# One core of a Trainium2 transformer layer: pooling input moved into the preparation's gap, box sums into the read-out, both directions' low-rank products together

## The chip, the cores and the metric

The kernel runs on one core of a Trainium2 chip. The metric is the device time of one execution in microseconds (us); before the change three executions took 1624.69, 1631.42 and 1635.77 us, median 1631.42.

## What is computed

One layer of a backbone over 512 latent tokens (a grid of 8 rows of 64) with 256 context tokens ahead of them, 1024 channels, in float32. Sub-layer 1 normalises and projects the tokens once, and feeds two mixers; sub-layer 2 is a mixture of 32 experts, two per token. The change touches sub-layer 1 and, by names of buffers alone, what follows. Cut to what matters:

```python
p = modulate(rmsnorm(h), shift, scale) @ w_in         # pooling | r, k, v, xw, xa, xg | gates
# pooling mixer, latent tokens, windows 2, 4, 8, 16, 128 channels each
d = box_mean(box_mean(grid, 1, win), 2, win) - u      # "box sums": one linear map of u
pool_y = (d @ pool_w[group]) * pool_scale
# time mixing, for each of the directions 0 (forward) and 1 (backward), 16 heads of 64
w_log = -softplus(-(w0[d] + tanh(xw[:, :, d]) @ w2[d])) - 0.5      # low rank, 64 to 1024
a     = sigmoid(a0[d] + xa[:, :, d] @ a2[d])                      # low rank, 64 to 1024
s     = s * decay + (s @ -kk) b + v k        # step by step through the tokens, s: 64x64 a head
y     = s @ r
out   = sum over d of group_norm(y) + bonus, times sigmoid(xg) @ g2
# merge
x = (sig(g0) * (pool_y @ pool_proj) + sig(g1) * (out @ rwkv_proj)) @ w_out
```

## The kernel before

The program is a row of stages, each a block with a barrier behind it: begin (L111, norms and the transposed tokens hT), low_rank_inputs (L230), prepare (L294), recurrence (L583), read_out (L967), pooling (L1091), merge (L1148), project_out (L1262), routing and experts. Inside a block each engine runs a list of its own and waits on semaphores that the others raise: TensorE (pe), VectorE (dve), ScalarE (act), GpSimd (pool), and SyncE (sp), which issues the DMAs in the order in which they are written.

Preparation runs over 8 groups m of 128 channels, as a hardware loop of four passes with two groups in each. For a group, TensorE makes k, the low-rank products a0 and a1 (`low`, L396), r, v, w0, w1, then the norm of k per head (L419) and the bonus (L423). The low-rank inputs xw and xa are [128, 2, 768]: one direction's 64 rows hold values and the other 64 are zero (memsets in L258), so each of the four is a product of all 128 rows. ScalarE turns banks of PSUM into k, r, v (`tap`, L441 to L443), sigmoids (`sig`, L451), and powers of the decay (Exp, L467 to L469); VectorE makes the running sums cum and cumx and the operands KR and BK (names pr_KR, pr_BK); SyncE stores them to DRAM (v at L349, KR and BK at L356), each group to a place of its own, in which a chunk of 64 tokens is a piece:

```python
g["kr_dram"] = dram("kr_chunks", [2, KT, CHUNKS * P * 2 * C])   # direction, group, chunk
```

The recurrence goes through 12 chunks of 64 tokens, 4 of context and 8 latent, in both directions at once. The list `recurrence_units` (L565) sets the order of TensorE's units of work and of those that read them; unit n uses bank slot n % 4. Per chunk SyncE loads BK, KR and V (L644, L650) in pieces of 512 and 256 bytes, and stores both directions' outputs y of latent chunks (L656). TensorE's parts: L703 products of operands, L710 transposes, L722 and L727 the state's products, L737 products of 64x64 blocks, L781 and L798.

The read-out reloads y of both directions (ro_y, 4 MB) and takes 16 tiles of 128 channels (8 groups, 2 directions) through rounds j: mean (TensorE, L1024), centring (VectorE, L1071), square (ScalarE, L1050), variance (TensorE, L1030), and for every second tile Ln and Exp of two variances (ScalarE, L1058, L1061), each with a load of its table. The pooling input u = hT x w_pool (32 products of 128x512, L1008, in four tiles of 8) is computed here: two tiles ahead of the rounds, the other two spread over the odd rounds, two products in each. The pooling block after it makes box sums (L1121, 4 products for each of the four windows) and the products with pool_w.

```python
for q in range(8): pool_input(q)                 # L1012: 16 products
for j in range(N + 5):
    if j < N and j % 2 == 1: pool_input(8 + j // 2)
```

The merge (L1208) takes 8 groups of 16 products for the gates and the two branches.

## Time and profile before

| what | value |
|---|---|
| median of 3 executions | 1631.42 us (1624.69 to 1635.77) |
| the profiled execution's own time | 1635.48 us |
| its span in the trace | 1633.5 us, mean granted clock of TensorE 0.927 |
| TensorE busy | 1362.1 us (83%), 16458 products |
| VectorE, ScalarE, GpSimd busy | 650.0 us, 583.9 us, 234.9 us |
| DMA packets | 169322, 285.62 MB |
| preparation's last product, recurrence's first | 381.9, 418.09 |
| read-out's first DMA issue | 896.96 |
| merge's first product | 1012.11 |

Read the table with the span's start as zero; the execution's own time is longer than the span by what lies around it. A busy share is an average over stages that have different limits, so the time of a stage, and which wait ends last in it, say more. A TensorE product in float32 leaves two records in the trace.

### The profile page before, as it was taken

What the parts mean: (1) busy time and instruction counts of PE and PEld (TensorE: products, weight loads), DVE (VectorE), ACT (ScalarE), POOL (GpSimd) and SP (SyncE); (2) the same over time, 40 slices, a digit from 0 to 9 for tenths busy, and PEclk for the clock granted to TensorE, in tenths of its full rate; (3) what the DMA queues carried; (4) which work ended last, traced back from release to release, by engine and by line L of the source; (5) the groups of instructions that cost most, each with busy time, mean ns of one, the idle gap of its engine ahead of it and who ended that gap; (6) DMA issues with size and microseconds to landing.
All of it is one profiled execution on the core that took longest, in us unless ns stands there. A gap on an engine that the chain in (4) does not pass through costs nothing. (4 is left out here: it accounts for less than half of the span.)

```text
span 1633.5 us, 37682 instructions
## 1 busy us (share of the span) xinstructions
PE 1362.1 (83%) x16458; PEld 821.5 (50%) x16458; DVE 650.0 (40%) x989; ACT 583.9 (36%) x880; POOL 234.9 (14%) x191
## 2 busy tenths in 40 slices
PE   5899999993698889999997887999999739887780
PEld 3445554551688888888886333344434423222220
DVE  1437676775355444444443162234233240000004
ACT  4225555543455555555553282000001211111113
POOL 0011111111322333333330000000000011000102
PEclk9999999997799999999999898999999859998895
DMA  8205444544523233222310505943429178999994
GB/s 353 84 6 167 137 129 129 154 112 113 130 69 82 78 78 85 81 81 81 81 42 32 221 1 220 378 163 132 188 71 383 51 297 340 426 425 425 424 366 180
DMA packets 169322, 285.62 MB, mean 175 GB/s; under 512 B 43332, under 2 KB 141764, under 8 KB 155092
## 3 DMA queue, kind: packets, MB, share of 16 engines
q1 hardware_dynamic: 163220, 254.00, 43.9%
q0 software_dynamic: 5952, 29.36, 4.7%
q8 instruction: 126, 2.06, 0.5%
q14 instruction: 24, 0.19, 0.0%
HBM read 236.14 MB, written 55.59 MB: 179 GB/s over the span
## 5 line engine op out<-in xcount | busy, mean ns | idle before, releaser
L390 PE MATMUL pr_ps<-hT,pr_w 128*128 128x512 f32 x384 | 173.4, 609 | 15.3 <-ACT pr_rate L451 10.7
L390 PEld LDWEIGHTS pr_ps<-hT,pr_w 128*128 128x128 f32 x384 | 74.0, 195 | 110.1 <-issue 89.7
L941 DVE COPY_PREDICATED rc_T<-masks_sb,rc_ps 128x512 f32<-128x512 uint32 x96 | 65.1, 729 | 161.3 <-PE rc_ps L737 161.3
L1208 PE MATMUL mg_ps<-hT,mg_w 128*128 128x512 f32 x256 | 111.2, 592 | 1.0 <-PEq L1102 1.0
L737 PE MATMUL rc_ps<-rc_T,rc_Z 64*64 64x64 f32 x3840 | 75.7, 222 | 15.5 <-issue 14.1
L703 PE MATMUL rc_ps<-rc_KR,rc_BK 64*128 64x128 f32 (+1 forms) x768 | 55.8, 292 | 37.1 <-DMA rc_KR<-kr_chunks 36.2
L1670 DVE TENSOR_TENSOR mg_w<-mg_w,ex_pgu 128x256 f32<-128x256 f32 x16 | 6.7, 421 | 191.5 <-ACT mg_w L1664 191.5
L1208 PEld LDWEIGHTS mg_ps<-hT,mg_w 128*128 128x128 f32 x256 | 48.6, 190 | 62.6 <-issue 62.6
L863 ACT ACTIVATE rc_Z<-rc_ps 128x1024 f32<-128x1024 f32 (+1 forms) x48 | 41.4, 880 | 104.5 <-PE rc_ps L703 104.5
L881 ACT ACTIVATE rc_G<-rc_ps 128x512 f32<-128x512 f32 x120 | 66.5, 599 | 32.9 <-PE rc_ps L737 32.4
L737 PEld LDWEIGHTS rc_ps<-rc_T,rc_Z 64*64 64x64 f32 x3840 | 65.9, 135 | 20.8 <-issue 16.1
L1227 ACT ACTIVATE mg_sig<-mg_ps 128x512 f32<-128x512 f32 x16 | 9.6, 597 | 183.8 <-PE mg_ps L1208 183.8
L1802 PE MATMUL ex_pgu<-ex_top,hT 128*32 128x512 f32 x240 | 68.2, 685 | 7.7 <-DMA hT<-in_w_experts 3.9
L487 POOL TENSOR_TENSOR pr_kd<-pr_rate,pr_kka 128x768 f32<-128x768 f32 x16 | 28.9, 1807 | 315.4 <-DVE pr_kraw L533 315.4
L710 PE MATMUL rc_ps<-masks_sb,rc_T 128*128 128x128 f32 x480 | 68.1, 283 | 5.5 <-DVE rc_Tf L939 5.5
L905 POOL TENSOR_TENSOR rc_Z<-rc_Z,masks_sb 64x512 f32<-64x512 f32 x48 | 64.4, 1342 | 49.0 <-ACT rc_Z L863 46.4
L703 PEld LDWEIGHTS rc_ps<-rc_KR,rc_BK 64*128 64x128 f32 x768 | 49.4, 199 | 41.6 <-issue 40.1
L883 ACT ACTIVATE rc_Tt<-rc_ps 128x512 f32<-128x512 f32 x120 | 66.9, 611 | 6.6 <-PE rc_ps L710 6.6
L737 PE MATMUL rc_ps<-rc_G,rc_Tt 64*64 64x64 f32 x3072 | 59.0, 222 | 7.8 <-issue 6.0
L1664 ACT ACTIVATE mg_w<-ex_pgu 128x256 f32<-128x256 f32 x16 | 6.1, 383 | 159.1 <-PE ex_pgu L1802 159.1
L1314 PE MATMUL po_ps<-pl_w_box,merged 128*128 128x512 f32 x128 | 60.6, 636 | 2.8 <-PEq L1163 2.8
L737 PEld LDWEIGHTS rc_ps<-rc_G,rc_Tt 64*64 64x64 f32 x3072 | 51.6, 135 | 15.3 <-issue 9.4
(338 smaller groups left out, 2669.9 us busy)
## 6 DMA issues: line engine op xcount, KB each, us to landing
bonus_sb<-in_ada_w SPq DMA_DIRECT2D x16, 1024.0 KB, 6.7
ex_top<-in_w_experts SPq DMA_DIRECT2D x8, 2048.0 KB, 18.5
mg_w<-in_w_merge SPq DMA_DIRECT2D x8, 1792.0 KB, 7.9
pr_w<-in_w_prep SPq DMA_DIRECT2D x8, 1664.0 KB, 6.6
kr_chunks<-pr_KR SPq DMA_DIRECT2D x16, 768.0 KB, 4.8
bk_chunks<-pr_BK SPq DMA_DIRECT2D x16, 768.0 KB, 6.8
rc_BK<-bk_chunks SPq DMA_DIRECT2D x24, 512.0 KB, 5.4
rc_KR<-kr_chunks SPq DMA_DIRECT2D x24, 512.0 KB, 5.4
```

Source lines behind the costliest of these rows:

```text
L390: last = pe.matmul(lat_bank[:, :], wv[:, j * KT + kt, :], hT[:, kt, lat], start=(kt == 0), stop=(kt == KT - 1))
L703: last = pe.matmul(out[:, b, j * P:j * P + w], BK[at, d, p, :, :].rearrange("p j t -> p (j t)"), KR[u][at, d, p, :, :].rearrange("p j t -> ...
L710: last = pe.transpose(out[:, q // Q, q % Q * P:q % Q * P + P], src(q), g["ident"])
L737: last = pe.matmul(out[to, k, q * C:q * C + C], lhs(at, q, s, b), rhs(at, q, s, b), start=True, stop=True)
L863: act.activation(Z[u][:, d // 2, :, at:at + Q, 0:w], src.rearrange("p b (j n) -> p b j n", n=P)[:, :, :, 0:w], ACT.Copy).then_inc(act_s, 1)
L881: act.activation(G[:, d, :, :, :], src[:, :, 0:Q * C].rearrange("p s (q t) -> p s q t", q=Q), ACT.Copy).then_inc(act_s, 1)
L883: act.activation(Tt[:, d, :, :, :], turned, ACT.Copy).then_inc(act_s, 1)
L905: pool.tensor_tensor(first, first, both[OWN[side], 0:C].unsqueeze(1).unsqueeze(1).to_broadcast([HD, 2, Q, C]), ALU.mult)
L941: dve.copy_predicated(T[u][:, d, :, :, :].rearrange("p q b t -> p b q t"), level(int(s[1:]), d), by_side).then_inc(dve_s, 1)
L1208: last = pe.matmul(ps[u][j][:, :], w[:, u, w0 + k, :], rhs, start=(k == 0), stop=(k == n - 1))
L1314: last = pe.matmul(ps[t % 2][:, h * 512:h * 512 + 512], merged[:, k, t * P:t * P + P], w[:, k, h * 512:h * 512 + 512], start=(k == 0), sto ...
L1802: last = pe.matmul(p_gu[v][rows, :], xT[:, v, k, rows], up(u)[:, k, :], start=(k == 0), stop=(k == KT - 1))
```

## The change

- **Low-rank products.** xw and xa become [128, 768], direction 0 in rows 0 to 63 and direction 1 in rows 64 to 127. a0 and a1 are made together, as products of 64 rows, and w0 and w1 likewise, into the same banks as before. The memsets and one copy each in low_rank_inputs go.
- **cumx and e_prev go.** KR's k part takes the decay power of the neighbouring column of e_in, and a copy of 12 columns fills the chunks' ends.
- **Layout of the operands in DRAM.** By chunk, then row, then group: [.., CHUNKS, P, KT, ..]. A load of a chunk has one piece of 4 KB (KR, BK) or 2 KB (v) a row; a store's pieces have the size that they had and lie 4 KB or 2 KB apart.
- **Pooling input.** w_pool is loaded into a new tile, pool_space, in two parts during the preparation. Three tiles (24 products) follow the loop, with ScalarE's copies, and the fourth opens the recurrence's block.
- **y of direction 1 stays on chip**, in the place of w_pool; direction 0 alone is stored and reloaded.
- **Read-out.** The first box sum stands ahead of the rounds; seven more steps (box sums and pool_w products in turn) stand in rounds 1, 3, ... 13, each waiting until ScalarE has copied the one before. The pooling block goes. sq, rs and diff live in tiles that the merge uses later. The merge's weights for its first group load at the end of the read-out's list, those for the second at the merge's start.
- **Names of buffers.** x_tiles, k_ka and k_rest move into pool_space; project_out's rows and f, and the experts' slots, take other tiles.

```diff
-        low_rank = {"a0": (1, g["xa"], 0, PAIR[1]), "a1": (1, g["xa"], 1, PAIR[0]), "w0": (0, g["xw"], 0, PAIR[0]), "w1": (0, g["xw"], 1, PAIR[1])}
+        low_rank = {"a": (1, g["xa"], (PAIR[1], PAIR[0])), "w": (0, g["xw"], (PAIR[0], PAIR[1]))}
...
+                            sp.dma_start(dst[d].rearrange("c p m n -> p c (m n)")[:, :, ds(mt2, 2 * C)],
...
+                sp.dma_start(g["w_pool"][:, LATE_K:, :], I["w_pool"][:, LATE_K:, :]).then_inc(g["wp_loaded"], 16)
                 for m in (KT - 2, KT - 1):
-                    store(m, m * NO, m * NV)
-                    store_operands(m, m * NO)
+                    store(m, m * C)
+                    if m == KT - 1:
+                        sp.wait_ge(pool_s, pool_o.value("kd1", m))
+                        sp.dma_start(g["w_pool"][:, 0:LATE_K, :], I["w_pool"][:, 0:LATE_K, :]).then_inc(g["wp_loaded"], 16)
+                    store_operands(m, m * 2 * C)
...
                         def low(name):
-                            maps, src, d, pair = low_rank[name]
+                            maps, src, pairs = low_rank[name]
                             for part, (a, n) in enumerate(parts):
-                                last = pe.matmul(pair[part][:, 0:n], wv[:, 3 * KT + maps, :], src[:, d, a:a + n], start=True, stop=True)
-                            pe_o.done(name, last)
-
+                                for d in range(2):
+                                    h = slice(HD * d, HD * d + HD)
+                                    last = pe.matmul(pairs[d][part][:, 0:n], wv[h, 3 * KT + maps, :], src[h, a:a + n], start=True, stop=True)
+                                    if part == 1:
+                                        pe_o.done(f"{name}{d}", last)
...
-                        low("a0")
-                        low("a1")
+                        low("a")
                         pe.wait_ge(act_s, act_o.value("sig_a0", m))
                         project("r")
                         pe.wait_ge(dve_s, dve_o.value("conv_v", m, 1))
                         project("v")
                         pe.wait_ge(act_s, act_o.value("sig_a1", m))
-                        low("w0")
                         pe.wait_ge(dve_s, dve_o.value("conv_r", m))
-                        low("w1")
+                        low("w")
                         pe.wait_ge(act_s, act_o.value("sig_w0", m))
...
+                pe.wait_ge(dve_s, dve_o.value("conv_v", KT - 1))
+                pe.wait_ge(g["wp_loaded"], 32)
+                for t in range(3):
+                    for j, k in enumerate([*range(LATE_K, KT), *range(LATE_K)]):
+                        last = pe.matmul(INPUT[t][:, :], hT[:, k, CTX + t * P:CTX + t * P + P], g["w_pool"][:, k, :], start=(j == 0), stop=(j == KT - 1))
+                    last.then_inc(g["u_made"], 1)
...
+                for t in range(3):
+                    act.wait_ge(g["u_made"], t + 1)
+                    act.activation(g["u"][:, t, :], INPUT[t][:, :], ACT.Copy)
...
-                            dve.tensor_tensor(KR[:, d, :, 0, :], chunks(kk[:, :]), chunks(e_prev[:, :]), ALU.mult)
+                            dve.tensor_tensor(KR[:, d, :, 0, later], chunks(kk[:, :])[:, :, later], chunks(e_in[:, :])[:, :, sooner], ALU.mult)
+                            dve.tensor_copy(KR[:, d, :, 0, end], chunks(kk[:, :])[:, :, end])
...
                 def load_pairs(dst, src, i, sem_):
                     for d in range(2):
-                        c = chunk_of(d, i)
-                        sp.dma_start(dst[:, d, :, :, :].rearrange("p i b t -> p i (b t)"),
-                                     src[d][:, c * NO:(c + 1) * NO].rearrange("i (p n) -> p i n", p=P)).then_inc(sem_, 16)
+                        sp.dma_start(dst[:, d, :, :, :].rearrange("p i b t -> p (i b t)"),
+                                     src[d, chunk_of(d, i)].rearrange("p i n -> p (i n)")).then_inc(sem_, 16)
...
                 def store(i):
-                    sp.wait_ge(dve_s, dve_at[("Y", i, 1)])
-                    for d in range(2):
-                        at = (chunk_of(d, i) - CTX_CHUNKS) * NY
-                        sp.dma_start(g["y_chunks"][d:d + 1, at:at + NY].rearrange("a (p n) -> (a p) n", p=P),
-                                     yc[i % 2][:, d, :, :, :].rearrange("p q s t -> p (q s t)")).then_inc(y_stored[i % 2], 16)
+                    sp.wait_ge(dve_s, dve_at[("Y", i, 0)])
+                    at = (chunk_of(0, i) - CTX_CHUNKS) * NY
+                    sp.dma_start(g["y_chunks"][0:1, at:at + NY].rearrange("a (p n) -> (a p) n", p=P),
+                                 yc[i % 2][:, :, :, :].rearrange("p q s t -> p (q s t)")).then_inc(y_stored[i % 2], 16)
...
+                t = SEQ // P - 1
+                for k in range(KT):
+                    last = pe.matmul(bank[:, 3, 0, :], g["hT"][:, k, CTX + t * P:CTX + t * P + P], g["w_pool"][:, k, :], start=(k == 0), stop=(k == KT - 1))
+                last.then_inc(g["u_made"], 1)
...
+                def pool_step(n):
+                    j = n // 2
+                    if n:
+                        pe.wait_ge(pool_read, n)
+                    if n % 2 == 0:
+                        pe.wait_ge(pb["boxed"][j], 16)
+                        for t in range(NT):
+                            last = pe.matmul(pooled[:, :], g["u"][:, t, j * P:j * P + P], pb["box"][:, j, t, :], start=(t == 0), stop=(t == NT - 1))
+                    else:
+                        if j == 0:
+                            pe.wait_ge(pb["pw_loaded"], 16)
+                        last = pe.matmul(pooled[:, :], pb["pw"][:, j, :], diff[:, j, :], start=True, stop=True)
+                    last.then_inc(pool_made, 1)
+                pool_step(0)
...
-                    if j < N and j % 2 == 1:
-                        pool_input(8 + j // 2)
+                    if j % 2 == 1 and j < 15:
+                        pool_step(j // 2 + 1)
...
+                def read_pool(n):
+                    j = n // 2
+                    act.wait_ge(pool_made, n + 1)
+                    if n % 2 == 0:
+                        act.activation(diff[:, j, :], pooled[:, :], ACT.Copy).then_inc(pool_read, 1)
+                    else:
+                        act.activation(py[:, j, :], pooled[:, :], ACT.Copy, scale=chan[:, 41 + j:42 + j]).then_inc(pool_read, 1)
+                read_pool(0)
...
-                    if j in (7, 15):
-                        read_input(2 + j // 8)
+                    if j % 2 == 1 and j < 15:
+                        read_pool(j // 2 + 1)
...
-        g["v_dram"] = dram("v_chunks", [KT, CHUNKS * P * C])
-        g["kr_dram"] = dram("kr_chunks", [2, KT, CHUNKS * P * 2 * C])
-        g["bk_dram"] = dram("bk_chunks", [2, KT, CHUNKS * P * 2 * C])
+        g["v_dram"] = dram("v_chunks", [CHUNKS, P, KT, C])
+        g["kr_dram"] = dram("kr_chunks", [2, CHUNKS, P, KT, 2 * C])
+        g["bk_dram"] = dram("bk_chunks", [2, CHUNKS, P, KT, 2 * C])
...
+        g["w_pool"] = space[:, 0:KT * 512].rearrange("p (k n) -> p k n", k=KT)
+        g["u"] = space[:, KT * 512:].rearrange("p (t n) -> p t n", n=512)
+        g["y1"] = space[:, 0:KT * 512].rearrange("p (c k t) -> p c k t", c=LAT_CHUNKS, t=C)
```

**First place.** TensorE in one group of the preparation, around w0 and w1, whose products read xw_sb. A row is an instruction or a run of equal ones. Before:

```order
L413 REGISTER_ALU
L399 MATMUL pr_ps<-xw_sb,pr_w 128x512
L399 MATMUL pr_ps<-xw_sb,pr_w 128x256
L415 REGISTER_ALU
L399 MATMUL pr_ps<-xw_sb,pr_w 128x512
L399 MATMUL pr_ps<-xw_sb,pr_w 128x256
L417 REGISTER_ALU
```

After:

```order
L413 REGISTER_ALU
L414 REGISTER_ALU
L400 MATMUL pr_ps<-xw_sb,pr_w 128x512 x2
L400 MATMUL pr_ps<-xw_sb,pr_w 128x256 x2
L416 REGISTER_ALU
L418 MATMUL pr_ps<-pr_ksq,masks_sb 128x512
```

The four products stand as two pairs of the same shape, and the wait that stood between w0 and w1 (L415) now stands ahead of both.

**Second place.** TensorE from the bonus product of the last group (pr_rkd) to the recurrence's first products (rc_KR). Before:

```order
L423 MATMUL pr_ps<-pr_rkd,pr_rk 128x512
L381 REGISTER_ALU
L381 COMPARE_AND_BRANCH
L337 UNCONDITIONAL_BRANCH
L678 UNCONDITIONAL_BRANCH
L703 MATMUL rc_ps<-rc_KR,rc_BK 128x64 x32
```

After, where pool_space holds w_pool:

```order
L422 MATMUL pr_ps<-pr_rkd,pr_rk 128x512
L379 REGISTER_ALU
L379 COMPARE_AND_BRANCH
L429 MATMUL pr_ps<-pool_space,hT 128x512 x24
L333 UNCONDITIONAL_BRANCH
L694 UNCONDITIONAL_BRANCH
L835 MATMUL rc_ps<-pool_space,hT 128x512 x8
L721 MATMUL rc_ps<-rc_KR,rc_BK 128x64 x32
```

24 products of the pooling input moved in ahead of the block's end, and 8 behind it.

**Third place.** ScalarE in the read-out's steady rounds. Before, where ro_sq holds the squares:

```order
L1050 ACTIVATE ro_sq<-ro_y 128x512 x2
L1058 ACT_TABLE_LOAD
L1058 ACTIVATE ro_rs<-ro_var,small_sb 128x512 x2
L1061 ACT_TABLE_LOAD
L1061 ACTIVATE ro_rs<-ro_rs 128x1024
L1050 ACTIVATE ro_sq<-ro_y 128x512 x2
```

After, where mg_w (sq, rs) and merged (diff) are the tiles that the merge uses later:

```order
L1085 ACTIVATE mg_w<-ro_y 128x512
L1085 ACTIVATE mg_w<-pool_space 128x512
L1093 ACT_TABLE_LOAD
L1093 ACTIVATE mg_w<-ro_var,small_sb 128x512 x2
L1096 ACT_TABLE_LOAD
L1096 ACTIVATE mg_w<-mg_w 128x1024
L1077 ACTIVATE pool_y<-ro_pool,chan_sb 128x512
L1085 ACTIVATE mg_w<-ro_y 128x512
```

The copy of a box sum (L1075) or of a pool_w product (L1077) now ends each pair of rounds, behind the Exp. On TensorE the step that this copy releases stands ahead of the mean of the next odd round:

```order
L1038 MATMUL ro_pool<-pl_w_box,pool_space 128x512 x4
L1054 MATMUL ro_mean<-pool_space,mean_w 128x512
L1060 MATMUL ro_var<-mg_w,mean_w 128x512
L1054 MATMUL ro_mean<-ro_y,mean_w 128x512
L1060 MATMUL ro_var<-mg_w,mean_w 128x512
L1042 MATMUL ro_pool<-merged,pl_pw 128x512
L1054 MATMUL ro_mean<-pool_space,mean_w 128x512
L1060 MATMUL ro_var<-mg_w,mean_w 128x512
L1054 MATMUL ro_mean<-ro_y,mean_w 128x512
```

## Rows read from the trace of the kernel before

**Rows 1.** The page's 40 equal slices of the span: TensorE's granted clock in tenths.
```profile
PEclk9999999997799999999999898999999859998895
```
**Rows 2.** Timeline of TensorE in the preparation: start us, us, instruction, records, [idle before <- what ended it].
```profile
172.93 15.70 PE L390 MATMUL pr_ps<-hT,pr_w 128*128 128x512 f32 x32 [2.04 <-ACT pr_rate L451]
...
323.32 14.00 PE L390 MATMUL pr_ps<-hT,pr_w 128*128 128x512 f32 x32 [2.04 <-ACT pr_rate L451]
...
355.85 2.74 PE L399 MATMUL pr_ps<-xa_sb,pr_w 128*128 128x512 f32 x8
359.52 14.00 PE L390 MATMUL pr_ps<-hT,pr_w 128*128 128x512 f32 x32 [0.93 <-ACT pr_rate L451]
...
380.80 1.09 PE L423 MATMUL pr_ps<-pr_rkd,pr_rk 128*128 128x512 f32 x2
```
**Rows 3.** Timeline of ScalarE in the preparation.
```profile
317.71 0.83 ACT L469 ACTIVATE pr_e<-pr_cumx 128x768 f32<-128x768 f32 x1
318.56 1.28 ACT L441 ACT_TABLE_LOAD   x1
...
322.21 1.99 ACT L451 ACTIVATE pr_rate<-pr_ps,pr_par 128x512 f32<-128x512 f32 x4
```
**Rows 4.** Timeline of SyncE's queue: DMA issues.
```profile
380.48 0.37 SPq L349 DMA_DIRECT2D v_chunks<-pr_v  x1
395.38 0.37 SPq L356 DMA_DIRECT2D kr_chunks<-pr_KR  x1
...
408.32 1.01 SPq L644 DMA_DIRECT2D rc_BK<-bk_chunks  x2
...
896.96 0.33 SPq L991 DMA_DIRECT2D pl_w_box<-in_w_pool  x1
```
**Rows 5.** Windows: 5 us of the gap; busy of five engines, granted clock, DMA share, GB/s.
```profile
400.00:405.00 5.00, 0.00 (x0) 0.00 (x0) 0.00 (x0) 0.00 (x0) 0.00 (x0) 0.50 1.04 282
```
**Rows 6.** Timeline of TensorE, first chunks of the recurrence, and one later row.
```profile
418.09 7.10 PE L703 MATMUL rc_ps<-rc_KR,rc_BK 64*128 64x64 f32 x64 [36.20 <-DMA rc_KR<-kr_chunks]
425.12 3.67 PE L710 MATMUL rc_ps<-masks_sb,rc_BK 128*128 128x128 f32 x16
443.11 2.00 PE L703 MATMUL rc_ps<-rc_KR,rc_BK 64*128 64x64 f32 x32
452.35 1.91 PE L710 MATMUL rc_ps<-masks_sb,rc_BK 128*128 128x128 f32 x16
...
555.37 2.06 PE L703 MATMUL rc_ps<-rc_KR,rc_BK 64*128 64x128 f32 x32
```
**Rows 7.** TensorE's waits over the span: us in total, times, longest us.
```profile
PE rc_ps L737 <- issue: 20.6, 21, 2.5
```
**Rows 8.** DMA issues: count, KB each, median us from issue to landing.
```profile
y_chunks<-rc_yc SPq DMA_DIRECT2D x16, 256.0 KB, 2.3
pl_w_box<-in_w_pool SPq DMA_DIRECT2D x1, 2048.0 KB, 8.3
```
**Rows 9.** Timeline of TensorE, read-out to merge.
```profile
905.32 9.60 PE L1008 MATMUL ro_pool<-pl_w_box,hT 128*128 128x512 f32 x16 [12.27 <-DMA pl_w_box<-in_w_pool]
922.57 1.02 PE L1024 MATMUL ro_mean<-ro_y,mean_w 128*128 128x512 f32 x2
949.72 3.78 PE L1008 MATMUL ro_pool<-pl_w_box,hT 128*128 128x512 f32 x4 [4.00 <-ACT pl_u L1041]
989.84 9.99 PE L1121 MATMUL pl_ps<-pl_w_box,pl_u 128*128 128x512 f32 x16 [3.81 <-PEq L988]
1012.11 13.97 PE L1208 MATMUL mg_ps<-hT,mg_w 128*128 128x512 f32 x32 [1.02 <-PEq L1102]
```
**Rows 10.** Timelines of ScalarE and VectorE in the read-out's rounds.
```profile
961.48 1.13 ACT L1050 ACTIVATE ro_sq<-ro_y 128x512 f32<-128x512 f32 x2
967.50 1.13 ACT L1050 ACTIVATE ro_sq<-ro_y 128x512 f32<-128x512 f32 x2
955.05 0.69 DVE L1071 TENSOR_TENSOR ro_y<-ro_y,ro_mean 128x512 f32<-128x512 f32 x1 [6.80 <-PE ro_mean L1024]
```

More of the change, by code:

```diff
@@ L256, in _ @@
             def _(dve):
-                for z in (xw, xa):
-                    dve.memset(z[:, :, :], 0.0)
-                dve.drain()
                 for j in range(3):
@@ L280, in _ @@
                 act.wait_ge(cv, 1)
-                for d in range(2):
-                    h = slice(64 * d, 64 * d + 64)
-                    act.activation(xw[h, d, :], y[h, 0, :], ACT.Tanh)
+                act.activation(xw[:, :], y[:, 0, :], ACT.Tanh)
                 act.wait_ge(cv, 3)
@@ L620, in recurrence @@
         two = lambda nm, s: [sb(f"{nm}{u}", s) for u in range(2)]
[L621 removed]
+        KR, Z, UV, BKt = two("KR", [KT, 2, C]), two("Z", [2, KT, 2 * C]), two("UV", [KT, 2, C]), two("BKt", [KT, 2, C])
+        yc = [ctx.enter_context(nc.sbuf_tensor(f"rc_yc{u}", [P, Q, 2, C], F32)) for u in range(2)]
         BK, V, S = sb("BK", [KT, 2, C]), sb("V", [KT, C]), sb("S", [KT, C])
@@ L980, in read_out @@
         varis = [ctx.enter_context(nc.psum_tensor(f"ro_var{k}", [P, SEQ], F32)) for k in range(4)]
-        inputs = ctx.enter_context(nc.psum_tensor("ro_pool", [P, 512], F32))
-        u_made, u_read = sem("ro_u_made"), sem("ro_u_read")
-        loaded, y_loaded = sem("ro_loaded"), [sem(f"ro_y{k}") for k in range(2)]
+        pooled = ctx.enter_context(nc.psum_tensor("ro_pool", [P, SEQ], F32))
+        pool_made, pool_read = sem("ro_pool_made"), sem("ro_pool_read")
+        loaded, y_loaded = sem("ro_loaded"), sem("ro_y0_loaded")
         mean_s, cen_s, sq_s, var_s, rs_s, yn_s = sem("ro_means"), sem("ro_centred"), sem("ro_squared"), sem("ro_vars"), sem("ro_rstd"), sem("ro_normed")
@@ L990, in _ @@
             def _(sp):
-                sp.dma_start(pb["w"][:, :, :], I["w_pool"]).then_inc(pb["loaded"], 16)
-                sp.dma_start(g2[:, :], I["g2"]).then_inc(loaded, 16)
-                for d in range(2):
-                    sp.dma_start(y[:, d, :, :, :].rearrange("p c k t -> p c (k t)"),
-                                 g["y_chunks"][d:d + 1, :].rearrange("a (c p n) -> (a p) c n", c=LAT_CHUNKS, p=P)).then_inc(y_loaded[d], 16)
-                sp.dma_start(pb["pw"][:, :, :], I["pool_w"]).then_inc(pb["pw_loaded"], 16)
@@ L997, in _ @@
-                for j in range(2):
-                    sp.dma_start(pb["box"][:, j, :, :], I["pool_box"][j]).then_inc(pb["boxed"][j], 16)
+                box = lambda j: sp.dma_start(pb["box"][:, j, :, :], I["pool_box"][j]).then_inc(pb["boxed"][j], 16)
+                box(0)
+                sp.dma_start(y0[:, :, :, :].rearrange("p c k t -> p c (k t)"),
+                             g["y_chunks"][0:1, :].rearrange("a (c p n) -> (a p) c n", c=LAT_CHUNKS, p=P)).then_inc(y_loaded, 16)
+                sp.dma_start(pb["pw"][:, :, :], I["pool_w"]).then_inc(pb["pw_loaded"], 16)
@@ L1000, in _ @@
+                sp.dma_start(g2[:, :], I["g2"]).then_inc(loaded, 16)
+                for j in range(1, 4):
+                    box(j)
+                next_loads(sp)
             @block.tensor
             def _(pe):
-                def pool_input(j):
-                    t = j // 4
-                    if j % 4 == 0 and t >= 1:
-                        pe.wait_ge(u_read, t)
-                    for k in (2 * (j % 4), 2 * (j % 4) + 1):
-                        last = pe.matmul(inputs[:, :], g["hT"][:, k, CTX + t * P:CTX + t * P + P], pb["w"][:, k, :], start=(k == 0), stop=(k == KT - 1))
-                    if j % 4 == 3:
-                        last.then_inc(u_made, 1)
@@ L1633, in experts @@
         dn = lambda u: ew[u][1].rearrange("p (k n) -> p k n", k=2)
-        got = [[small["top"][:, (2 * t + j) * D:(2 * t + j + 1) * D] for j in range(2)] for t in range(NT)]
-        sq = small["top"][:, 2 * NT * D:(2 * NT + 1) * D]
-        x1, acc = (ew[u][0].rearrange("p (t n) -> p t n", t=NT) for u in (5, 1))
-        gt, gain = (ew[5][1][:, q * D:(q + 1) * D] for q in range(2))
+        units = [part[:, q * D:(q + 1) * D] for u in (4, 5) for part in ew[u] for q in range(part.shape[1] // D)]
+        got, sq = [units[2 * t:2 * t + 2] for t in range(NT)], units[2 * NT]
+        x1, acc = (ew[u][0].rearrange("p (t n) -> p t n", t=NT) for u in (6, 1))
+        gt, gain = (ew[6][1][:, q * D:(q + 1) * D] for q in range(2))
         y_spill = got[0][0]
```

172 lines of the change are left out of this document (66 added, 106 removed).

## The prediction

> **What bounds the kernel now.** I first read the busy shares on the page: TensorE is busy for 83% of the span, twice as long as any other engine. So up to the experts the question is what TensorE waits for; all changed parts lie ahead of them, where a shorter stage moves everything behind it. Then the page's line of the granted clock: it stands at 9 in most slices and falls to 7, and once to 5, so the array doesn't run at one speed [rows 1].
>
> Next the timeline of TensorE and ScalarE in the preparation, one channel group after another (the four low-rank products stand with 8 records, since each product leaves two). TensorE leads, but at two places in each group it goes at ScalarE's pace. The k product ends, the low-rank products of a run (355.85, 2.74 us), and r starts at 359.52 only, 0.93 idle. What ends that wait is the first pair of sigmoids (half of the four in 1.99), and ahead of it on ScalarE stand k's two taps and then a table load of 1.28 [rows 2, 3]. Norm stands in the same way behind w0's sigmoids.
>
> The gap between preparation and recurrence: the last product of the preparation ends at 380.80 + 1.09 = 381.9, called T below. The last operands are stored from 395.38, the next block's first load is issued at 408.32, and the recurrence's first product starts at 418.09, after 36.20 idle on DMA [rows 2, 4, 6]. In the stores the DMA engines are full at 282 GB/s and TensorE's granted clock is 0.50, its lower level of 1.2 GHz [rows 5]. The recurrence starts at that level: 64 records of L703 take 7.10, later 32 take 2.00; 16 transposes 3.67, later 1.91 [rows 6].
>
> Last the read-out. Its w_pool load is waited for (12.27), mean products start at 922.57, the pooling block's first product at 989.84, the merge's at 1012.11 [rows 9]. In steady state ScalarE sets the pace: two squares every 967.50 - 961.48 = 6.02 [rows 10].
>
> **Price of a product and of a cold start.** 32 records in 14.00 are 16 products, 0.875 each at 2.4 GHz [rows 2]. After 12.27 idle 8 products took 9.60 in place of 7.0; after 4.00 idle 2 took 3.78 in place of 1.75; after 3.81 idle 8 took 9.99 [rows 9]. So a start at 1.2 GHz costs 2.0 to 3.0; I take 2.6. In the preparation r and v together are 14.00 warm. After 2.04 idle they took 15.70 in two groups and 14.00 in a third: 1.7 more, in two of three; after 0.93 they were warm [rows 2].
>
> **1. Low-rank products, both directions at once: nothing from the products, +2.4 in all.** In the recurrence 16 products of 64 rows over 128 columns take 2.06, where 8 of 128 rows take 1.91: two of 64 rows run beside each other [rows 6]. So 2.74 becomes about 1.4, twice in each of 8 groups. But r still waits for a0's sigmoid behind taps and table load, and norm for w0's: TensorE's 1.3 a time turn into idle time. The idle time ahead of r grows from 0.93 to 2.2 in every group, as long as the 2.04 that left r cold in two of three. That is 8 x 1.7 x 2/3 = +9.1 (bounds 0 and 13.6), less the 2 x 1.7 already paid: +5.7. Against it, cumx and one Exp per direction go (0.83 each on ScalarE, one subtraction on VectorE). Now ScalarE ends the last Exp at 317.71 + 0.83 and then loads a table (1.28) before k's tap [rows 3]; with 1.7 of Exp less, that load lies beside the k product. I estimate 1.1 of it won, in the three groups where it is late now: -3.3. The twelve-column copy into KR is hidden on VectorE. Sum +2.4; bounds -6.7 and +6.9. The memset and one of two copies ahead of the preparation I take at nothing (0 to -0.5).
>
> **2. The gap: -3.7.** TensorE gets 24 products of the pooling input. Its weights' last part (768 KB) is issued behind v's store of 380.48; 2048 KB took 8.3 [rows 8], so 768 KB behind that store some 5: T + 4.3. From there 24 x 0.875 = 21.0, 2.6 for the cold start, and 1.1 for the last copy and the change of block: T + 29.0. The stores started at T + 13.5 and were done 12.9 later, at 408.32 [rows 4]; with the shorter chain ahead of them I take both 1.5 earlier, T + 24.9, so they are hidden by 4; that is what they may slow down by. Then the fourth tile, 8 products, 7.0: T + 36.3. The first loads took 9.8 from issue to product (418.09 - 408.32) [rows 4, 6]; in lines of 4 KB instead of 512 B I take 8, so they land about when it ends. The first recurrence product starts at T + 36.7, before at T + 36.2: +0.5. But warm: (7.10 - 4.00) + (3.67 - 1.91) = 4.9 less, of which I take 4.2, since masks and T then come late. Bounds of the whole: -6 and +4 (cold again).
>
> **3. The recurrence: -5.** No product moves. TensorE waits there 20.6 in 21 pieces on "issue" in L737 alone, up to 2.5 each [rows 7]: it has the next product's inputs and no instruction. I suspect instruction fetch, held back by the loads' many small lines, on the same DMA engines. A load now has an eighth of the lines, and half of y's stores go. I take a quarter of the 20.6, -5; bounds 0 and -15, and above zero in a rival.
> The Trainium skill (Runtime: NRT & Kernel Launch, Instruction fetch mechanics) has the instruction stream fetched in 16 KiB blocks over a DMA queue, the cost of a boundary "mostly hidden". The trace doesn't agree with "mostly hidden", if these waits are fetches: 20.6 us [rows 7]. By the page this term is 0 and the sum -8.1.
> The last store of the stage is one transfer behind one direction's add: -1.2 (0 to -2), half of 2.3, the time of a transfer of 256 KB, two of which it was [rows 8].
>
> **4. Read-out and pooling, 896.96 to 1012.11, 115.1 us: now about 107, -8.2; merge +2.6.** B is the block's start. The first box (1 MB; 2 MB took 8.3 [rows 8]) is there at B + 5.0; four products, cold, 3.5 + 2.6: means start at B + 11.1, before at 922.57 - 896.96 = 25.6 [rows 4, 9]. So 14.5 are won, and the pooling block's 22.3 go. But the box sums don't fill a hole. Steps 1 to 7 stand in the odd rounds, and each but the first waits for ScalarE's copy of the step before, which ScalarE does at the end of a round, behind Ln and Exp. So a round with a pooling step becomes a chain: step P, mean 0.88, centring 0.69, square 0.57, Ln and Exp with their tables 967.50 - 961.48 - 1.13 = 4.89, copy 0.69, hand-offs 0.4: 8.1 + P [rows 3, 10]. P is 3.5 (box sums) or 0.88 (pool_w): 11.6 or 9.0, where the old loop took 6.02.
> Step 1 waits for the copy of step 0 alone and adds nothing; step 2 stands in the fourth round, 5.0 behind the first mean product, B + 16.1. From there 11.6 + 9.0 + 11.6 + 9.0 + 11.6 = 52.8 to step 7. Behind it 9.0 for its round, 6.0 for the last pair, 4.9 for Ln and Exp and 4.3 for VectorE's last six operations (up to 0.69 each, with hand-offs): 24.2 [rows 10]. Sum B + 93.1. In each of five rounds TensorE then waits 3.8 for ScalarE, and after 3.81 and 4.00 it was cold each time [rows 9]: 5 x 2.6 = 13.0. B + 106.1, and 0.8 to the merge: 106.9. The bound without a cold round is 94, with the lower clock all the way 113.
> The merge started warm behind the pooling block (16 products 13.97 [rows 9]). Now TensorE has waited some 4 us for VectorE's tail: +2.6. Merge weights of m = 1 now load beside its first round of 27 us: hidden. The experts' slots change names, not numbers: nothing.
>
> **Sum.** 2.4 - 3.7 - 5 - 1.2 - 8.2 + 2.6 = -13.1. The profiled execution took 1635.5 (span 1633.5), so it would be 1622.4 in its frame; it lay 4.1 above the median of the runs, 1631.4. I forecast 1618. About 1% (16 us) is what a measurement of this kernel can tell from no change.
>
> **Rivals.**
> - The read-out stays warm. For it: there are products in each round, and r stayed warm once after 2.04. Against: no wait of 3.8 or more in the trace was followed by a warm start. It gives 13 more: 1605.
> - The lower clock through the whole loop, since TensorE works little more than half of each round. 113 instead of 106: 1625.
> - The fetch waits don't hang on the loads: term 3 is 0, 1623. This is also what the page of the Trainium skill named above gives.
> - The row pairs don't run together: w0 is then done after 512, 512 and 256 columns, 0.86 later than now, in front of its sigmoid: 8 x 0.86 = 6.9, 1625. Or the stores, now scattered in lines of 512 B that lie 4 KB apart, run at half of 282 GB/s [rows 5]: 3 MB take 11 us more, 4 of it hidden: +7, 1625. The 2.06 of the recurrence speaks against the one [rows 6]; nothing against the other.
> - The slower side: lines of 4 KB hold the next instructions back longer than lines of 512 B. Place: the dense 64x64 products of the recurrence. If each of the 21 waits grew to the longest one now, 2.5 [rows 7], they'd be 52.5 in place of 20.6: +31.9, and with the other terms at -8.1 that is 1655. The kernel gets slower from 8.1 more on, a mean wait of 1.4 (now 0.98). Against it: the bursts get shorter.
>
> **How the numbers follow.** Forecast 0.40 (own range 1611 to 1626), warm read-out 0.20 (1598 to 1611), no fetch gain 0.13, lower clock throughout 0.10, pairs or stores 0.10, slower fetch 0.07. Faster by over 1%: the warm one and the lower part of the forecast's range, 0.38. Slower by over 1%: most of the last, 0.06. The rest, 0.56, is within 1%. The range takes in both bounds of the clock and leaves the slow fetch and an all-warm kernel outside: 1598 to 1638.
>
> **What would show it.** r starts some 3.5 behind k's end as before, with 2 us idle ahead of it, and reads 15.7 in most groups. 24 pooling products from about T + 4, 8 more ahead of L721, then 64 records of it in about 4. Rounds of 9 and 11.6 (warm) or 11 and 14 (cold) between pooling steps, TensorE waiting on ScalarE's copy of ro_pool ahead of each. "issue" in the 64x64 products about 15. Merge some 9 earlier against the read-out's start. Wrong if the rounds stay at 6 to 8, if r starts earlier behind k, or if "issue" grows.

## The result and the profile after

The changed kernel took 1613.8 us (median of four, 1606.39 to 1617.86) against 1630.14 us of the kernel before: ratio 0.9894, 95% interval 0.9844 to 0.9944. The forecast was 1618. Its profiled execution took 1617.86 us with a span of 1615.8, 17.7 less than the 1633.5 of before. The stages below are cut at the same events in both traces, so they add up to these 17.7.

| stretch | before | after | difference | forecast |
|---|---|---|---|---|
| span's start to the preparation's first product | 83.6 | 85.3 | +1.7 | 0 |
| to the end of the last bonus product | 298.3 | 301.9 | +3.6 | +2.4 |
| to the recurrence's first product | 36.2 | 37.9 | +1.7 | +0.5 |
| recurrence, first to last product | 475.0 | 460.4 | -14.6 | -9.2 (-4.2 warm start, -5 issue) |
| to the read-out's first DMA issue | 3.9 | 3.7 | -0.2 | -1.2 |
| read-out and pooling, to the merge's first product | 115.2 | 101.5 | -13.7 | -8.2 |
| merge to the end | 621.4 | 625.2 | +3.8 | +2.6 |

First TensorE's timeline in two groups of the preparation, the gap, and the recurrence's start, as [rows 2, 6].

```profile
212.56 15.70 PE L388 MATMUL pr_ps<-hT,pr_w 128*128 128x512 f32 x32 [2.02 <-ACT pr_rate L459]
...
288.60 14.00 PE L388 MATMUL pr_ps<-hT,pr_w 128*128 128x512 f32 x32 [2.02 <-ACT pr_rate L459]
302.44 3.62 PE L391 MATMUL pr_ps<-hT,pr_w 128*128 128x256 f32 x16
305.99 1.56 PE L400 MATMUL pr_ps<-xw_sb,pr_w 64*128 64x512 f32 x8
308.68 1.56 PE L418 MATMUL pr_ps<-pr_ksq,masks_sb 128*128 128x512 f32 x4 [1.14 <-ACT pr_s L459]
...
391.73 23.72 PE L429 MATMUL pr_ps<-pool_space,hT 128*128 128x512 f32 x48 [4.58 <-DMA pool_space<-in_w_pool]
416.38 7.10 PE L835 MATMUL rc_ps<-pool_space,hT 128*128 128x512 f32 x16 [0.93 <-PEq L333]
425.06 3.79 PE L721 MATMUL rc_ps<-rc_KR,rc_BK 64*128 64x64 f32 x64 [1.58 <-DMA rc_KR<-kr_chunks]
428.78 1.97 PE L728 MATMUL rc_ps<-masks_sb,rc_BK 128*128 128x128 f32 x16
...
434.03 0.69 PE L755 MATMUL rc_ps<-rc_T,rc_Z 64*64 64x64 f32 x32 [2.31 <-DVE rc_T L958]
434.65 1.61 PE L728 MATMUL rc_ps<-masks_sb,rc_T 128*128 128x128 f32 x8
436.06 1.91 PE L728 MATMUL rc_ps<-masks_sb,rc_V 128*128 128x128 f32 x8
```

The pair of low-rank products takes 1.56 in place of 2.74 (so two row halves do run at once), and both waits behind it have grown: 2.02 ahead of r in all eight groups (before, 0.93 in five and 2.04 in three), 1.14 ahead of norm, where there was none. The row of r, with v's latent products in it, reads 15.70 in five groups and 14.00 in three. The gap holds its 24 and 8 products; L721 takes 3.79 in place of 7.10, but then TensorE waits 2.31 for VectorE, and behind that wait its clock falls: the granted clock is 0.50 from 436 to 437, and the two rows of transposes take 1.61 and 1.91, where before they took 1.09 and 1.04. The window's columns are length, busy time of TensorE, its weight loads, VectorE, ScalarE and GpSimd, granted clock, DMA share and GB/s.

```profile
436.00:437.00 1.00, 1.00 (x7) 1.00 (x6) 0.00 (x0) 0.64 (x2) 0.91 (x1) 0.50 0.04 16
```

Then what TensorE waited for on "issue", and how the recurrence as a whole reads (columns as above); the first row is of before, the second of after.

```profile
PE rc_ps L755 <- issue: 11.3, 17, 2.0
PE rc_ps L816 <- issue: 5.3, 4, 1.6
PE rc_ps L799 <- issue: 4.2, 5, 1.6
```

```profile
418.09:893.04 474.95, 432.35 (x12832) 396.31 (x12832) 223.75 (x299) 265.11 (x448) 137.48 (x97) 0.98 0.28 73
```

```profile
425.06:885.46 460.40, 426.52 (x12832) 390.79 (x12832) 222.67 (x299) 265.18 (x448) 137.98 (x97) 0.99 0.21 70
```

L755 is the L737 of before, whose issue waits were 20.6 [rows 7]. Over all lines they went from 33.0 to 22.5; TensorE is busy 5.8 less with the same 12832 records, and waits 2.3 more for VectorE. On SyncE's queue the recurrence's first load stands 29.2 behind the bonus product:

```profile
416.34 0.83 SPq L662 DMA_DIRECT2D rc_BK<-bk_chunks  x2
```

The read-out: TensorE's steps 2 to 7 with the wait ahead of each, the merge's first products, then ScalarE around one copy, and two windows (columns as above), as [rows 9, 10].

```profile
905.27 3.70 PE L1038 MATMUL ro_pool<-pl_w_box,pool_space 128*128 128x512 f32 x8 [0.30 <-ACT pool_y L1077]
...
916.94 2.08 PE L1042 MATMUL ro_pool<-merged,pl_pw 128*128 128x512 f32 x2 [4.53 <-ACT merged L1075]
...
927.51 6.62 PE L1038 MATMUL ro_pool<-pl_w_box,pool_space 128*128 128x512 f32 x8 [3.77 <-ACT pool_y L1077]
...
942.10 1.12 PE L1042 MATMUL ro_pool<-merged,pl_pw 128*128 128x512 f32 x2 [3.67 <-ACT merged L1075]
...
951.28 6.68 PE L1038 MATMUL ro_pool<-pl_w_box,pool_space 128*128 128x512 f32 x8 [3.76 <-ACT pool_y L1077]
...
965.93 1.13 PE L1042 MATMUL ro_pool<-merged,pl_pw 128*128 128x512 f32 x2 [3.67 <-ACT merged L1075]
...
990.64 16.07 PE L1194 MATMUL mg_ps<-hT,mg_w 128*128 128x512 f32 x32 [3.17 <-PEq L1015]
```

```profile
914.05 1.28 ACT L1096 ACT_TABLE_LOAD   x1
915.34 1.06 ACT L1096 ACTIVATE mg_w<-mg_w 128x1024 f32<-128x1024 f32 x1
916.30 0.58 ACT L1075 ACTIVATE merged<-ro_pool 128x512 f32<-128x512 f32 x1
```

```profile
942.00:948.00 6.00, 5.42 (x12) 2.20 (x12) 3.29 (x6) 3.50 (x6) 0.00 (x0) 1.00 0.01 3
...
951.00:957.00 6.00, 5.72 (x7) 2.52 (x8) 0.00 (x0) 0.74 (x2) 0.00 (x0) 0.50 0.00 0
```

Each step starts where ScalarE's copy of the step before ends, and the copy stands behind Ln and Exp. From step to step it is 11.7, 10.6, 14.6, 9.2, 14.7. The box sums at 927.51 and 951.28 took 6.62 and 6.68, where those of step 2 took 3.70: they ran for the most part at the lower level of 1.2 GHz (granted clock 0.50 in the second window), the products at 942.10 at 2.4 GHz (1.00).

### The profile page after: what moved, and what is told of

It reads as the page before. It is cut to its first block and busy times, and to the rows that moved or that the text cites. A ratio compares the mean times of both kernels' runs of the same rounds, so it can differ in the third digit from the quotient of the medians.

```text
span 1615.8 us, 37637 instructions
## 1 busy us (share of the span) xinstructions
PE 1353.4 (84%) x16458; PEld 808.5 (50%) x16458; DVE 629.2 (39%) x982; ACT 572.2 (35%) x867; POOL 235.9 (15%) x191
## 3 DMA queue, kind: packets, MB, share of 16 engines
q8 instruction: 126, 2.06, 0.5%
## 5 line engine op out<-in xcount | busy, mean ns | idle before, releaser
L388 PE MATMUL pr_ps<-hT,pr_w 128*128 128x512 f32 x384 | 179.3, 626 | 20.2 <-ACT pr_rate L459 16.2
L755 PE MATMUL rc_ps<-rc_T,rc_Z 64*64 64x64 f32 x3840 | 74.4, 222 | 11.1 <-issue 7.1
L497 POOL TENSOR_TENSOR pr_kd<-pr_rate,pool_space 128x768 f32<-128x768 f32 x16 | 29.0, 1810 | 316.9 <-DVE pr_kraw L543 316.9
L755 PEld LDWEIGHTS rc_ps<-rc_T,rc_Z 64*64 64x64 f32 x3840 | 65.1, 135 | 17.4 <-issue 9.6
L755 PE MATMUL rc_ps<-rc_G,rc_Tt 64*64 64x64 f32 x3072 | 58.1, 222 | 4.0 <-issue 2.5
L391 PE MATMUL pr_ps<-hT,pr_w 128*128 128x256 f32 x256 | 57.9, 379 | 0.0
L728 PEld LDWEIGHTS rc_ps<-masks_sb,rc_T 128*128 128x128 f32 x480 | 52.3, 143 | 11.0 <-DVE rc_Tf L964 6.8
L1194 PE MATMUL mg_ps<-rwkv_y,mg_w 128*128 128x512 f32 x128 | 57.7, 604 | 0.0
L755 PEld LDWEIGHTS rc_ps<-rc_G,rc_Tt 64*64 64x64 f32 x3072 | 51.0, 135 | 11.4 <-issue 5.6
## 6 DMA issues: line engine op xcount, KB each, us to landing
rwkv_y<-in_w_experts SPq DMA_DIRECT2D x5, 2048.0 KB, 17.7
```

The costliest lines, as they stand in the source:

```text
L388: last = pe.matmul(lat_bank[:, :], wv[:, j * KT + kt, :], hT[:, kt, lat], start=(kt == 0), stop=(kt == KT - 1))
L391: last = pe.matmul(ctx_bank[:, 0:CTX], wv[:, j * KT + kt, :], hT[:, kt, 0:CTX], start=(kt == 0), stop=(kt == KT - 1))
L497: pool.tensor_tensor(kd[:, d, :], rate[:, d, :], k_ka[:, :], ALU.mult)
L728: last = pe.transpose(out[:, q // Q, q % Q * P:q % Q * P + P], src(q), g["ident"])
L755: last = pe.matmul(out[to, k, q * C:q * C + C], lhs(at, q, s, b), rhs(at, q, s, b), start=True, stop=True)
L1194: last = pe.matmul(ps[u][j][:, :], w[:, u, w0 + k, :], rhs, start=(k == 0), stop=(k == n - 1))
```

## The experiments

Nine kernels ran. Ratios are against the kernel before, on the same chip.

### Where the read-out's time is: copy_first

```diff
                 for j in range(N + 2):
+                    if j % 2 == 1 and j < 15:
+                        read_pool(j // 2 + 1)
                     if j < N:
...
                             act.activation(two, two, ACT.Exp, scale=-0.5).then_inc(rs_s, 2)
-                    if j % 2 == 1 and j < 15:
-                        read_pool(j // 2 + 1)
```

> The changed kernel with one edit: ScalarE copies a pooling step's bank at the start of an odd round, ahead of the square, instead of behind Ln and Exp. Theory (the chain through Ln and Exp sets the pace of the rounds with a step): from step 2 to step 7 the changed kernel took 60.7 us in five pairs of rounds; now a pair goes at ScalarE's own pace or TensorE's, 6.7 to 8, so 34 to 40 us, with no cold start in it; 20 to 27 us less in all, some 1590 us. Rival (TensorE's added products and its lower clock set the pace): the pairs stay at 9 to 14 us and the time at 1614.

Measured: 1588.29 us, ratio 0.9727 (0.9692 to 0.9763). From step 2 to step 7 TensorE took 34.6 us, and the read-out 76.0 instead of 101.5. Its timeline at these two steps:

```profile
900.92 3.67 PE L1038 MATMUL ro_pool<-pl_w_box,pool_space 128*128 128x512 f32 x8
...
935.55 1.02 PE L1042 MATMUL ro_pool<-merged,pl_pw 128*128 128x512 f32 x2
```

No wait stands ahead of either, and no step between them was cold. So the chain through Ln and Exp was the pace, and the 25 us were for the place of one small copy on ScalarE; 7.3 of them were the cold products of steps 3, 4 and 6, which went with the waits. The rival is out.

### What the pairs of low-rank products gave: pairs_alone

The kernel before with `low` and its inputs as in the diff of the change, nothing else.

> The kernel before with the low-rank products made for both directions at once, and nothing else of the change. Theory (r and norm wait for sigmoids that stand behind taps and a table load): groups stay at 36.2 and 37.3, the idle ahead of r grows by 1.1 in each, and more groups are cold at 1.7 each: 0 to 9 us more than before. Rival (TensorE's products are the path): 16 x 1.2 = 19 us less.

Measured: 1632.64 us, ratio 1.0015 (1.0001 to 1.0030). The preparation took 300.6, 2.3 more than before.

```profile
174.37 14.00 PE L383 MATMUL pr_ps<-hT,pr_w 128*128 128x512 f32 x32 [3.01 <-ACT pr_rate L446]
```

TensorE's time turned into waits nearly one for one: 3.01 ahead of r here, where it was 2.04, and 2.02 in the other groups, where it was 0.93. The row above is warm behind its 3.01; in the two other groups with that wait, and in one of the five with 2.02, it read 15.65 to 15.70. Starts of r are 36.33 or 37.31 apart, 1.7 more where products were cold. In the changed kernel all eight groups are 36.33 but for that, so leaving out cumx and its Exp is worth the 1.0 in three groups, as far as these two kernels show; none leaves out cumx alone.

### Does idle time make r cold: filler_r

```diff
                         low("a")
+                        pe.wait_ge(dve_s, dve_o.value("conv_v", m, 1))
+                        for _ in range(2):
+                            pe.matmul(B_V[:, :], wv[:, 0, :], hT[:, 0, lat], start=True, stop=True)
                         pe.wait_ge(act_s, act_o.value("sig_a0", m))
```

> The changed kernel with work added that nobody reads: two products of 128x512 (1.72 us) behind the low-rank products of a, in the 2.02 us in which TensorE waits ahead of r. Theory (r reads 15.70 instead of 14.00 in five of eight groups because TensorE stood idle): the idle falls to about 0.3, r starts when it did, and is warm in all eight groups: 8.5 us less, in spite of 14 us of products more. Rival (the lower clock has another cause): no change, within 2 us; r stays at 15.7 in some groups.

Measured: 1601.61 us, ratio 0.9828 (0.9807 to 0.9849). The preparation took 293.4 instead of 301.9.

```profile
209.69 1.02 PE L411 MATMUL pr_ps<-hT,pr_w 128*128 128x512 f32 x2
210.82 14.00 PE L388 MATMUL pr_ps<-hT,pr_w 128*128 128x512 f32 x32
```

All eight groups take 36.33 and no r is cold: 5 x 1.7 = 8.5, as expected. In all six kernels that have the changed kernel's preparation, the changed one among them, r was cold in five of eight groups, though not in the same five. The 16 added products, whose result nobody reads, make the kernel faster.

### The same in the read-out: filler_gates

```diff
+                        for _ in range(3 if j < 14 else 0):
+                            pe.matmul(gates[:, :], g2[:, k * P:k * P + P], g["xg"][:, :], start=True, stop=True)
                         pe.matmul(gates[:, :], g2[:, k * P:k * P + P], g["xg"][:, :], start=True, stop=True).then_inc(gate, 1)
```

> The changed kernel with the gate product of rounds 6, 8, 10 and 12 of the read-out made four times instead of once (2.6 us more each, same result). Theory (box sums of steps 4 and 6 take 6.6 instead of 3.5 since TensorE stood idle for 3.8 ahead of them): the idle falls to about 1.1, both take 3.6, the read-out gets 6 us shorter. Rival: nothing changes, steps 4 and 6 stay at 6.6 and the read-out at 101.5.

Measured: 1606.2 us, ratio 0.9851 (0.9825 to 0.9877); the read-out took 96.7, 4.7 less; 6 were expected. Steps 4 and 6:

```profile
920.88 3.70 PE L1038 MATMUL ro_pool<-pl_w_box,pool_space 128*128 128x512 f32 x8 [1.20 <-ACT pool_y L1079]
...
941.73 3.70 PE L1038 MATMUL ro_pool<-pl_w_box,pool_space 128*128 128x512 f32 x8 [1.19 <-ACT pool_y L1079]
```

Both are warm, 3.70 for 6.62 and 6.68. Step 3, ahead of which no filler stood, was cold still, and its cold products lasted somewhat longer (step 3 to step 4 took 11.7 for 10.6). In five other kernels with the changed kernel's read-out (filler_r, low_early, no_gap, old_layout, y_stores) it took 102.3 to 103.6, so 101.5 is at the short end. In low_early step 5, warm in the changed kernel (1.12), was cold behind the same wait:

```profile
909.94 1.84 PE L1047 MATMUL ro_pool<-merged,pl_pw 128*128 128x512 f32 x2 [3.67 <-ACT merged L1080]
```

### Can the waits of the preparation be taken away: low_early, and both edits together

`low("a")` stands between k's latent and context products, `low("w")` between v's, and on ScalarE:

```diff
-                        tap("k", "kraw")
                         sig("a0")
                         sig("a1")
+                        tap("k", "kraw")
...
-                        tap("v", "bonus")
                         sig("w0")
                         sig("w1")
+                        tap("v", "bonus")
```

> The changed kernel with the low-rank products of a moved between k's latent and context products, and those of w between v's, and ScalarE's sigmoids ahead of the tap of k and of v. Theory (TensorE waits 2.02 ahead of r and 1.14 ahead of norm in each group for sigmoids behind taps and a table load, and the 2.02 makes r cold in five of eight groups): a group takes 33.2 us instead of 36.3 or 38.0, both waits are gone, no cold start; 25 + 8.5 = 33 us less, some 1580 us. Rival (ScalarE's and VectorE's own chain through the group is as long as TensorE's, so the wait only moves to another place, to v's or the bonus product): 0 to 10 us less.

Measured: 1589.25 us, ratio 0.9737 (0.9704 to 0.9769). The preparation took 273.9, 28.0 less. The wait ahead of norm is gone; ahead of r something is left from the second group on:

```profile
130.83 5.42 PE L388 MATMUL pr_ps<-hT,pr_w 128*128 128x512 f32 x12 [0.83 <-ACT pr_rate L464]
```

```profile
127.58 0.83 ACT L480 ACTIVATE pr_e<-pr_cum 128x768 f32<-128x768 f32 x1
128.43 1.28 ACT L464 ACT_TABLE_LOAD   x1
129.72 1.99 ACT L464 ACTIVATE pr_rate<-pr_ps,pr_par 128x512 f32<-128x512 f32 x4
```

ScalarE's last Exp of the group before ends at 128.4, and the table load behind it still holds the sigmoid: a group is 34.1, not 33.2. Another part went back in the gap, 39.3 instead of 37.9: w_pool's last part is issued behind v's store, which now comes later behind v's products, and TensorE waits 7.47 for it (4.58 in the changed kernel). The rival was right in this: a part of the wait only moved.

> The edits of copy_first and low_early together. Theory: the stages are apart, so the gains add: 53 to 60 us less than the changed kernel, some 1557 us. Rival: one of them is lost in later waits (the merge or the experts, which would then wait for weights): less than 45.

Measured: 1564.64 us, ratio 0.9588 (0.9555 to 0.9621), 49 us below the changed kernel. That is about the sum of the two edits as measured (25.5 and 24.6) and less than what was expected of them (53 to 60); no third stage took anything back. It is the fastest kernel of this study.

### What the layout in DRAM gave: old_layout

The changed kernel with v, KR and BK stored and loaded by the lines of the kernel before.

> The changed kernel with the old layout of v, KR and BK in DRAM, so that loads have pieces of 512 and 256 bytes again and stores are contiguous. Theory (many small pieces of loads hold the instruction stream back): TensorE's waits on issue in the recurrence go from 22.4 back towards 33 us and the stage gets 8 to 12 us longer; with the first loads 1 us later, some 1624 us. Rival (the layout does nothing to issue, the gain of the stage came from its warm start and from y's missing stores): issue stays at 22, the time within 2 us of 1614.

Measured: 1626.06 us, ratio 0.9951 (0.9934 to 0.9969). Waits, the recurrence's window (as above), and the DMA view, then one row of the changed kernel's DMA view:

```profile
PE rc_ps L759 <- issue: 15.0, 19, 1.8
PE rc_ps L803 <- issue: 6.9, 5, 3.0
PE rc_ps L820 <- issue: 5.0, 4, 1.5
```

```profile
422.21:891.04 468.83, 428.69 (x12832) 392.88 (x12832) 223.12 (x299) 264.74 (x448) 137.75 (x97) 0.99 0.27 70
```

```profile
rc_KR<-kr_chunks SPq DMA_DIRECT2D x24, 512.0 KB, 5.3
```

```profile
rc_KR<-kr_chunks SPq DMA_DIRECT2D x24, 512.0 KB, 4.3
```

The recurrence got 8.4 us longer, and issue went from 22.5 to 30.0 over all lines. With the same bytes the DMA share is 0.27 for 0.21. In all eight kernels of the study with long lines issue lies between 16.9 and 22.5 (mean 20.5), in all three with short ones between 30.0 and 33.0 (mean 31.1). So short lines cause some 10 of the 33 us; old_layout, the only run in which nothing else differs, gives 7.5. Whether it is the number of lines or the time for which the DMA engines are busy isn't told apart. That the waits are instruction fetch is an argument too: the trace shows that TensorE had its inputs and nothing to run, and the page of instruction queues is no finer.

### y's stores: y_stores

```diff
-                    sp.wait_ge(dve_s, dve_at[("Y", i, 0)])
+                    sp.wait_ge(dve_s, dve_at[("Y", i, 1)])
+                    c1 = chunk_of(1, i) - CTX_CHUNKS
+                    sp.dma_start(g["y_chunks"][1:2, c1 * NY:(c1 + 1) * NY].rearrange("a (p n) -> (a p) n", p=P),
+                                 g["y1"][:, c1, :, :].rearrange("p k t -> p (k t)")).then_inc(y1_stored, 16)
```

> The changed kernel, which also stores y of direction 1 of each latent chunk, as before (nobody reads it back). Theory (the gain of the recurrence comes from the layout of the loads and from the warm start, y's missing stores have little part in it): the recurrence from its first product to its last stays within 1.5 us of the changed kernel's 460.4, TensorE's waits on issue at 19 to 23, and the block ends up to 1.2 us later behind the last product. Rival (stores of 256 KB hold the instruction stream back as loads do): issue 24 or more, the stage 2 to 5 us longer.

Measured: 1613.33 us, ratio 0.9911 (0.9885 to 0.9936).

```profile
PE rc_ps L760 <- issue: 6.5, 12, 1.1
```

The recurrence took 453.7, less than the changed kernel's 460.4, with issue at 16.9 over all lines; the block ended 3.94 behind the last product for 3.72. The run also says how far issue moves from one kernel to the next for no reason in the edit: the six kernels with the changed kernel's recurrence have 18.7 to 22.5, and this one, with more to store, 16.9. If the stores cost anything, it is less than this swing.

### What the products in the gap cost: no_gap

```diff
-                    for j, k in enumerate([*range(LATE_K, KT), *range(LATE_K)]):
+                    for j, k in ((0, LATE_K), (KT - 1, LATE_K - 1)):
...
-                for k in range(KT):
+                for k in (0, KT - 1):
```

> The changed kernel with 24 of the 32 products of the pooling input left out (two of eight are kept in each tile, so the pooling input is not the reference's). Theory (they stand beside the last stores and loads, and keep the clock up): the recurrence's first product starts 2 to 4 us earlier behind the bonus product than the 37.9 of the changed kernel, but its first products are cold (L721 about 7, transposes 3.7), so the whole is within 3 us of the changed kernel. Rival (they stand on the path): 10 to 15 us less.

Measured: 1611.04 us, ratio 0.9886 (0.9862 to 0.9910).

```profile
408.67 3.59 PE L835 MATMUL rc_ps<-pool_space,hT 128*128 128x512 f32 x4 [13.30 <-PEq L333]
417.47 7.10 PE L721 MATMUL rc_ps<-rc_KR,rc_BK 64*128 64x64 f32 x64 [5.21 <-DMA rc_KR<-kr_chunks]
424.50 3.67 PE L728 MATMUL rc_ps<-masks_sb,rc_BK 128*128 128x128 f32 x16
```

The recurrence starts 33.4 behind the bonus product, 4.5 earlier than in the changed kernel, and cold. From there to its last product it takes 459.4, one less than the warm start's 460.4. One us is less than what issue alone moves from kernel to kernel, so the stage's length doesn't show what the warm start buys. Its first hand-offs do: from the first product of L721 to the first of `rc_G` no_gap takes 14.0, the changed kernel 12.8, and the other kernels with all the products 11.5 to 13.1. Nor is 4.5 a firm price: in those whose preparation ends as the changed kernel's does, with long lines, the recurrence starts 35.4 to 37.6 behind the bonus product. So 24 products cost 2.0 to 4.5 us of path here and give 0.9 to 2.5 back. In the place that they had before, the read-out, the first 16 of the 32 and the load ahead of them made up the first 25.6 us.

## Why the forecast was right, and where not

The time lay 4 us below the forecast and in its own range of 1611 to 1626, and the kernel is faster by about 1%; the interval of the ratio, 0.9844 to 0.9944, lies on both sides of that bound. By the steps:

1. **Low-rank products (+2.4; measured +3.6).** The mechanism held as it was put: nothing from the products, r at the sigmoid's pace, cold in some groups. Five of eight r's were cold, for 5.3 in the estimate; pairs_alone shows that the products give nothing, filler_r that the wait makes r cold. Leaving out cumx gave 2.9 for 3.3. The rest is 0.8 in the first group, whose k was cold for longer, and 0.1 a group. One reading behind it was wrong: the row of 1.91 that the working takes as 8 products of 128 rows is 16 transposes, which leave one record each. The conclusion stands all the same: at 0.875 for 512 columns, 16 products of 128 columns one after another would take 3.5 by estimate, and they took 2.06; and here the pair took 1.56 for 2.74.
2. **The gap (-3.7; measured about +0.8).** The start at T + 36.7 came 1.2 late, the stores ended in time (no_gap: first load at T + 24.6; the estimate was T + 24.9), and scattered lines cost nothing (a store of KR took 4.7 for 4.8, of BK 6.8 as before): the rivals on stores and, by the 1.56 for 2.74, on the pairs fall. But the warm start of 4.2 was the wrong size. From the first product of L721 to the first of `rc_G`, before took 13.7 and the changed kernel 12.8: 0.9. The products were 5.0 faster, and then TensorE waited 2.6 for VectorE and ran the next transposes at the lower clock, 1.4 longer. I had allowed 0.7 for that. A faster piece was counted at its own time instead of at the next hand-off.
3. **The recurrence (-5; measured -10.5 in issue).** A quarter of L737's waits was too little: they fell from 20.6 to 11.3, the other lines' by 1.2, and over all lines 33.0 went to 22.5. old_layout shows that the layout is the cause of most of it, 7.5; the size of the term was a guess that came out at half. The rest of the 14.6 is TensorE's busy time, 5.8 less, of which the first products of point 2 gave 3.6, against 2.3 more of waits for VectorE. Fewer long waits may also mean fewer cold products behind them, but no run takes that apart. The Trainium skill's "mostly hidden" (Runtime: NRT & Kernel Launch, Instruction fetch mechanics) would have left the stage alone; if the waits are fetches, the trace goes against it with 33.0 us before and 22.5 after. The rivals "slower fetch" and "no fetch gain" fall.
4. **The last store (-1.2; measured -0.2).** The three kernels with both transfers (before, pairs_alone, y_stores) end the block 3.9 behind the last product, the eight with one 2.4 to 3.7, 3.3 on average. So the term is 0.7 on average and was 0.2 in this trace.
5. **Read-out (-8.2; measured -13.7).** The chain was right, to 0.3 us: step 2 at B + 16.1 as forecast, warm steps 11.7 and 9.2 for 11.6 and 9.0, tail 24.7 for 25.0. The five cold rounds at 2.6 = 13.0 were mis-sized: three were cold, by 1.4, 2.9 and 3.0, and steps 2 to 7 took 60.7, 7.9 more than the 52.8 of the warm chain. Steps 5 and 7 stayed warm after a wait of 3.67. In front of them TensorE had worked for 10.9 us at a stretch, in front of 4 and 6 for 6.8 and 5.4; step 3, behind a wait of 4.53, was cold after 18. Which rounds are cold is not fixed by the code: in four of the five other kernels with this read-out, step 5 too ran in part at the lower clock behind the same 3.67 (step 5 to 6 took 10.5 to 10.9 for 9.2, as in the row of low_early under filler_gates), and the whole took 103.0 to 103.6 for 101.5. So the part of this term's miss that belongs to the one trace is about 2 of the 5.5. "Warm read-out" and "lower clock throughout" both fall as rivals.
6. **Merge (+2.6; measured +3.8).** Its first 16 products took 16.07 for 13.97, the cold start that was forecast, and a wait for VectorE further on was 5.07 for 3.04, which was not.

What had not been in the sum at all: +1.7 ahead of the preparation, from products whose code is the same (below). Summed over the table's stretches the terms erred by +6.3 and by -10.9, which leaves -4.6: the mechanisms held, but that the time came closer than its terms is luck.

## What to carry to other kernels

Work that is moved into a pipelined loop is priced at the place of its hand-off: a copy of 0.6 us behind Ln and Exp made 12 us out of 7 for a pair of rounds, and moving it cost nothing and gave 25. Making an engine's work shorter where it waits for another engine gave nothing here, and on TensorE it cost, since the longer waits were followed by work at the lower clock more often; first move the other engine's step (here the sigmoid ahead of the tap). Loads in long lines helped not only the load: with them TensorE's waits on issue, in dense small products, were a quarter to a third shorter.
